# Latent scores in three products of high and low parts, and casts in slot order at two feed-forward fronts

## What is computed

```python
def _attend_blocks(q, k, v):            # q: 512 x 16 x 96, k: 768 x 16 x 96
    scale = QK_HEAD_DIM ** -0.5
    def one(qblk):                      # 128 queries
        s = jnp.einsum('bqhd,bkhd->bhqk', qblk, k, preferred_element_type=jnp.float32) * scale
        p = jax.nn.softmax(s, axis=-1).astype(v.dtype)
        return jnp.einsum('bhqk,bkhv->bqhv', p, v)
    ...
def _conv_ffn(h, w_up, conv_w, conv_b, w_down):
    gate, val = jnp.split(h @ w_up, 2, axis=-1)
    return (jax.nn.silu(_dwconv3(gate, conv_w, conv_b)) * val) @ w_down
```

## Time and profile before

| | |
|---|---|
| median of 3 runs | 3225.2 us (3224.78 to 3226.74) |
| the profiled execution | 3222.23 us |
| its span in the trace | 3220.4 us |
| PE busy | 3148.1 us, 98% |
| DVE, ACT, POOL busy | 62%, 46%, 43% |
| latent items | 997.6 to about 1230 us of the span |

### The profile page before, as it was taken

How to read it: one execution, slowest core, us unless ns; L and a number is a source line. 1 busy time by engine, 2 the same in 40 slices (tenths; PEclk the granted TensorE clock), 3 DMA queues, 4 the chain that set the end, 5 groups by cost and what they waited for, 6 DMA issues and landing times.

```text
span 3220.4 us, 45656 instructions
## 1 busy us (share of the span) xinstructions
PE 3148.1 (98%) x18262; PEld 2618.2 (81%) x18262; DVE 2003.2 (62%) x3212; ACT 1483.0 (46%) x2689; POOL 1382.0 (43%) x800
## 2 busy tenths in 40 slices
PE   7999999999999999999999999999999999989998
PEld 4876888888875557899986888899997788869997
DVE  5877366323337663877735685388873678368885
ACT  4323422222246774555544535455553544445554
POOL 2221423232254445355552234646555234435555
PEclk9999999999999999999999999999999999999999
DMA  7333334122132002223332120423333121213331
GB/s 272 109 97 120 126 101 151 56 63 69 50 118 103 14 14 88 90 92 105 112 122 75 47 67 34 129 79 100 104 118 107 44 71 45 63 57 105 100 99 68
DMA packets 89408, 288.53 MB, mean 90 GB/s; under 512 B 10187, under 2 KB 13835, under 8 KB 88428
## 3 DMA queue, kind: packets, MB, share of 16 engines
q1 hardware_dynamic: 89196, 285.60, 27.6%
HBM read 283.47 MB, written 2.10 MB: 89 GB/s over the span
## 4 chain that ended last, share of the span: by engine, by line
PE 82%; DVE 6%; issue 4%; POOL 4%; ACT 3%; DMA 1%; SPq 0%; POOLq 0%; DVEq 0%; ACTq 0%
PE ps L613 13%; PE ps L616 13%; PE ps L614 13%; PE ps L3432 6%; PE ps L3434 5%; PE ps L3433 5%; PE ps L672 2%; PE ps L674 2%; PE ps L673 2%; PE ps L2254 2%; POOL WL L561 1%; PE ps L3106 1%; DMA ring<-in_w_mod 1%; POOL T L904 1%; PE ps L2697 1%
## 5 line engine op out<-in xcount | busy, mean ns | idle before, releaser
L561 POOL TENSOR_TENSOR WL<-ring,WH 128x1024 fp32r<-128x1024 f32 (+4 forms) x477 | 975.2, 2050 | 1331.5 <-ACT WH L551 1331.5
L551 ACT CAST WH<-ring 128x1024 fp32r<-128x1024 f32 (+4 forms) x524 | 462.6, 884 | 442.1 <-PE ps L616 287.8
L613 PE MATMUL ps<-FR,WH 128*128 128x512 f32 x1120 | 419.5, 375 | 0.3
L614 PE MATMUL ps<-FR,WH 128*128 128x512 f32 x1120 | 410.2, 373 | 0.0
L616 PE MATMUL ps<-FR,WL 128*128 128x512 f32 x1120 | 389.2, 373 | 0.0
L613 PE MATMUL ps<-HX,WH 128*128 128x512 f32 x744 | 294.3, 396 | 0.0
L616 PE MATMUL ps<-HX,WL 128*128 128x512 f32 x744 | 292.7, 393 | 0.0
L614 PE MATMUL ps<-HX,WH 128*128 128x512 f32 x744 | 291.2, 391 | 0.0
L3432 PE MATMUL ps<-XH,WH 128*128 128x256 f32 x912 | 260.4, 285 | 10.5 <-ACT ps L3583 7.9
L3433 PE MATMUL ps<-XL,WH 128*128 128x256 f32 x912 | 258.7, 284 | 0.0
L3434 PE MATMUL ps<-XH,WL 128*128 128x256 f32 x912 | 258.6, 284 | 0.0
(11 more groups left out here) (465 smaller groups left out, 7480.4 us busy)
## 6 DMA issues: line engine op xcount, KB each, us to landing
ring<-in_ffn_w_up SPq DMA_DIRECT2D x88, 512.0 KB, 3.7
ring<-in_w_up SPq DMA_DIRECT2D x88, 512.0 KB, 3.7
ring<-in_w_mod SPq DMA_DIRECT2D x64, 512.0 KB, 4.4
ring<-in_w_in_tok SPq DMA_DIRECT2D x40, 512.0 KB, 3.7
ring<-in_w_mod_columns SPq DMA_DIRECT2D x32, 512.0 KB, 4.4
ring<-in_w_in_feat SPq DMA_DIRECT2D x32, 512.0 KB, 3.6
ring<-in_w_down SPq DMA_DIRECT2D x48, 320.0 KB, 4.0
ring<-in_ffn_w_down SPq DMA_DIRECT2D x40, 320.0 KB, 3.0
```

The source lines that it names most:

```text
L551: act.copy(WH[:, p % SPLITS, 0:n], src).then_inc(*split.a.up("high", p))
L561: pool.tensor_tensor(WL[:, p % SPLITS, 0:n], unit_source(p)[0], WH[:, p % SPLITS, 0:n], ALU.subtract).then_inc(*low_up(split.g, p))
L613: pe.matmul(o, high, xh, first, False)
L614: pe.matmul(o, high, xl, False, False)
```

## The change

Two changes that don't touch each other come together.

**Scores.** QT and KT become F32R, and hold the high parts. QL and KL, the low parts of the queries and keys of one batch, lie in the slots of WH and WL (all three of WL, two of WH). The one float32 product becomes three F32R products. ACT now casts queries and the first 512 keys of every head (`head_high`), DVE the last 256 keys, and DVE makes all three low parts (`head_low_v`), from PSUM and the high part. Since the slots are taken, `ring.upto` keeps the units of w_o from being asked for until step (11, 0), i = 51; three are cast by ACT at i = 64 and made low by POOL behind the last scaling, and PE's pieces of w_o move to (15, 0) and (15, 2), i = 67 and 69.

**Fronts.** In both early feed-forwards the unit of group 5 is made low by DVE instead of POOL (in `between(2)`), ACT's casts of units first + 6 to first + 8 move forward, and the rest and sums of (3) and (4) change places with the taps on DVE.

```diff
         in_vector |= {g_.last for t_ in (L_ffn1, *L_ffb) for g_ in (*t_.groups[3:5], *t_.groups[-8:])}
-        in_vector.add(L_ffb[1].groups[2].last)
+        in_vector |= {L_ffb[1].groups[2].last, L_ffb[1].groups[5].last, L_ffn1.groups[5].last}
...
-        QT = [buf(7360, 4, 512), buf(15680, 4, 512)]
-        KT = [buf(9408, 4, 768), buf(17728, 4, 768)]
+        QT = [nc.alloc_sbuf_tensor_at(f"QT{x}", [128, 4, 512], F32R, offset=base + 4 * o)
+              for x, o in enumerate((7360, 15680))]
+        KT = [nc.alloc_sbuf_tensor_at(f"KT{x}", [128, 4, 768], F32R, offset=base + 4 * o)
+              for x, o in enumerate((9408, 17728))]
+        QL = WH[:, :, :].rearrange("p a b -> p (a b)")[:, 0:2048].rearrange("p (a b) -> p a b", a=4)
+        KL = WL[:, :, :].rearrange("p a b -> p (a b)").rearrange("p (a b) -> p a b", a=4)
         VT = [buf(5824, 6, 256), CX[:, :, :].rearrange("p a b -> p (a b)")[:, 0:1536].rearrange("p (a b) -> p a b", a=6)]
         OT = buf(20800, 8, 512)
...
+            ring.upto = L_a.groups[-1].last + 1
...
-                cast_to(act, g.last + 2)
+                cast_to(act, min(g.last + 2, L_a.groups[-1].last))
...
-            cast_to(act, g.last + 3)
...
-            for g in L_a.groups:
-                rest_to(pool, g.last + 2)
-            rest_to(pool, g.last + 3)
+            rest_to(pool, L_a.groups[-1].last)
...
-        def heads_evict(eng, copy, W, n, h, odd):
-            for x, (src, ts, dst) in enumerate(turns(h)):
-                if (3 * h + x) % 2 == odd and (n or x):
-                    eng.wait_ge(*mla.pe.at("turn", n, h, x))
-                    copy(dst(n % 2), ps("turn", n, h, x)[0:96, 0:len(ts) * 128]).then_inc(
-                        *bank.emptied(("turn", n, h, x), W))
+        LAST_OF = (5, 7, 13, 15)
+
+        def head_high(eng, copy, W, n, h, x):
+            ts, dst = turns(h)[x][1:3]
+            eng.wait_ge(*mla.pe.at("turn", n, h, x))
+            copy(dst(n % 2), ps("turn", n, h, x)[0:96, 0:len(ts) * 128]).then_inc(*W.up("head high", n, h, x))
+
+        def head_low_v(dve, n, h, x):
+            ts, dst, lo = turns(h)[x][1:4]
+            if n:
+                dve.wait_ge(*att.pe.at("scores", 16 * n - 16 + LAST_OF[h], 1))
+            else:
+                dve.wait_ge(*split.pe.at("used", L_a.groups[-1].last))
+            dve.wait_ge(*(mla.a if x < 2 else mla.v).at("head high", n, h, x))
+            dve.tensor_tensor(lo, ps("turn", n, h, x)[0:96, 0:len(ts) * 128], dst(n % 2), ALU.subtract).then_inc(
+                *bank.emptied(("turn", n, h, x), mla.v))
 
...
             for h in range(4):
-                heads_evict(act, act.copy, mla.a, n, h, 1)
-                mla.a.mark("made", n, h)
+                for x in range(n == 0, 2):
+                    head_high(act, act.copy, mla.a, n, h, x)
...
+            if n == 0:
+                for h in range(4):
+                    head_low_v(dve, 0, h, 0)
             yield
             for h in range(4):
-                heads_evict(dve, dve.tensor_copy, mla.v, n, h, 0)
+                for x in range(n == 0, 2):
+                    head_low_v(dve, n, h, x)
+                head_high(dve, dve.tensor_copy, mla.v, n, h, 2)
+                head_low_v(dve, n, h, 2)
...
             c0, c1 = CUTS[j]
             pe.wait_ge(*mla.v.at("made", n, h))
-            pe.wait_ge(*mla.a.at("made", n, h))
             b = bank.take_in(f"scores{j}", "ls", i, j)
             pe.wait_ge(*bank.free("ls", i, j))
-            pe.matmul(PS[b][:, 0:c1 - c0], QT[n % 2][0:96, h, t * 128:t * 128 + 128], KT[n % 2][0:96, h, c0:c1], True,
-                      True).then_inc(*att.pe.up("scores", i, j))
+            o, rows_ = PS[b][:, 0:c1 - c0], slice(t * 128, t * 128 + 128)
+            pe.matmul(o, QT[n % 2][0:96, h, rows_], KT[n % 2][0:96, h, c0:c1], True, False)
+            pe.matmul(o, QT[n % 2][0:96, h, rows_], KL[0:96, h, c0:c1], False, False)
+            pe.matmul(o, QL[0:96, h, rows_], KT[n % 2][0:96, h, c0:c1], False, True).then_inc(*att.pe.up("scores", i, j))
 
...
                     bank.release("scores0")
                     bank.release("scores1")
-                if v >= 14 and part == 0:
+                if (v, part) == (11, 0):
+                    ring.upto = None
+                    ring.ask(ring.p + SPLITS)
+                if (v, part) in ((15, 0), (15, 2)):
                     next(out)
                     bank.kept.update(bank.place[L_o.name, g.key, 0] for g in L_o.groups[:2])
...
+                else:
+                    act.wait_ge(*att.pe.at("scores", 63, 1))
+                    cast_to(act, L_o.groups[2].last)
...
+                if i == 64:
+                    rest_to(pool, L_o.groups[2].last)
```

The fronts:

```diff
-            if not L.early:
+            if L.early:
+                between(2)
+            else:
                 between(0)
                 between(1)
             low(2)
...
                 center(0, 1)
+            if L.early:
+                cast_to(act, first + 6)
             gate_silu(0)
+            if L.early:
+                cast_to(act, first + 7)
             for n in range(1, FRONT):
                 if n >= 2:
                     high(n - 2)
                     if L.early:
-                        cast_to(act, first + 7)
+                        cast_to(act, first + 8)
                 center(n, 0)
                 gate_silu(n)
...
-            sums_1_2(FRONT + 1)
+            if not L.early:
+                sums_1_2(FRONT + 1)
             for n in range(FRONT):
                 for val in range(2):
                     key = (name, ("up", 2 * n + val), 0)
                     if not val or L.val_conv:
                         taps(n, val, ps(*key), key, T[:, 2 * val + n % 2, :])
-                    if n == (1 if L.early else FRONT - 1) and not val:
+                    if n == FRONT - 1 and not val and not L.early:
                         rest_v(dve, L.unit["1 2", FRONT])
                         sums_3_4(FRONT)
                 dve.wait_ge(*fw.v.now())
...
                         *bank.emptied(key, fw.v, "gated", name, n, 0))
+                if n == 0 and L.early:
+                    rest_v(dve, L.unit["1 2", FRONT])
+                    sums_3_4(FRONT)
                 if 1 <= n < FRONT - 1:
                     low(n - 1)
+                    if L.early:
+                        sums_1_2(FRONT + 1)
             for i in range(FRONT, FT + 1):
                 j = i - 1
                 if FRONT < i < FT:
```

More of the change, by code:

```diff
@@ L213, in start @@
     def start(self):
-        self.n, self.p, self.asked, self.cast, self.rest = 0, 0, 0, 0, 0
+        self.n, self.p, self.asked, self.cast, self.rest, self.upto = 0, 0, 0, 0, 0, None
     def raw(self, src, n, parts=128, kept=False):
@@ L234, in ask @@
     def ask(self, upto):
-        while self.asked < min(upto, len(self.splits)):
+        while self.asked < min(upto, len(self.splits) if self.upto is None else self.upto):
             src, n = self.splits[self.asked]
@@ L2035, in turns @@
         def turns(h):
-            return [(qtok, range(4), lambda g: QT[g][0:96, h, :]),
-                    (ktok, range(4), lambda g: KT[g][0:96, h, 0:512]),
-                    (ktok, range(4, 6), lambda g: KT[g][0:96, h, 512:768])]
+            return [(qtok, range(4), lambda g: QT[g][0:96, h, :], QL[0:96, h, :]),
+                    (ktok, range(4), lambda g: KT[g][0:96, h, 0:512], KL[0:96, h, 0:512]),
+                    (ktok, range(4, 6), lambda g: KT[g][0:96, h, 512:768], KL[0:96, h, 512:768])]
         def batch(x):
@@ L2092, in turned_heads_pe @@
         def turned_heads_pe(pe, n, h, x, what):
-            src, ts, dst = turns(h)[x]
+            src, ts = turns(h)[x][0:2]
             b = bank.take("turn", n, h, x)
@@ L2133, in heads_a @@
                 for h in range(4):
-                    act.wait_ge(*mla.pe.at("turn", 0, h, 0))
-                    act.copy(turns(h)[0][2](0), ps("turn", 0, h, 0)[0:96, :]).then_inc(
-                        *bank.emptied(("turn", 0, h, 0), mla.a))
+                    head_high(act, act.copy, mla.a, 0, h, 0)
             yield
             for h in range(4):
-                heads_evict(act, act.copy, mla.a, n, h, 1)
-                mla.a.mark("made", n, h)
+                for x in range(n == 0, 2):
+                    head_high(act, act.copy, mla.a, n, h, x)
                 yield
```

## The result

The changed kernel takes 3250.5 us (median of 4 runs, 3250.2 to 3254.1), the kernel before 3225.0 in the same comparison: ratio 1.0082, 95% interval 1.0070 to 1.0094. It is slower by 25.5 us, where the forecast was +19.6 and 3245.

A forecast was written before the change was run, and what follows sets the result against it. The latent stage was taken as bound by PE, busy 98% of the span. Terms -16.3 + 29.5 + 3.8 + 1.7 + 4.8 + 0.9 - 4.8 = +19.6 on 3225.2 gave 3245 us, range 3226 to 3262.

The forecast's parts named there:

- part 2: Items that make a head: DVE, ACT, DVE become a loop of 5.85 us an item; over three batches +29.5 us.
- sum pair: DVE's sum of the item before, queued behind the subtractions, counted as the last 0.25 us of the head items' loop.
- the hold: In the head items' loop, POOL's scaling delays DVE's combined maximum, which takes 0.59 us, 0.37 of it from contention.
- part 1: Latent score products: three F32R products replace the float32 pair, saving 0.255 us an item on PE, 64 times, -16.3 us.
- part 3: Start of the latent items: batch 0's casts and subtractions precede item 0, +3.8 us; half clock behind PE's idle, +1.7.
- part 4: End of the latent items: w_o waits for POOL's low parts and a moved piece comes later, +4.8 us; half clock, +0.9.
- part 5: Early fronts: the wait for POOL goes, the copy's wait grows; copies come 3.0 and 3.5 us earlier, -4.8 us altogether.
- The heads were not absorbed: Rival for the head items: PE has enough work ahead to hide the loop, part 2 is nil, 3215.5 us; chance 0.10.
- the F32R products of an item: Rival for the scores: three F32R products take as long as the float32 pair, part 1 is nil, 3261 us; chance 0.05.
- PE's clock did fall in the head items: Rival: half clock in the head items adds 2.4 to 13.2 us, middle 8, three times, giving 3269 us; chance 0.09.

## Why the prediction was right, point by point

**The loop** (part 2) was right as a mechanism and, to a few hundredths, in size: 5.85 us an item counted, 5.85 measured, and 5.85 + 6.00 + 6.33 + 5.85 = 24.03 from item 28 to 32 where 24.0 stood. What PE gets back behind it was put at 1.0 and is 1.3 (item 17 at 1.83 us instead of 3.16). The three head stages, items 12 to 17 of each batch, cost 8.5 us net in the trace; the sum had 9.8 less the saving of five items, 8.5. Taking the sum pair and the hold out of the loop shortened it by just what they last (0.26 and 0.38), and taking the exponentials out left an item at DVE's own work.

**The scores** (part 1) are the term that was mis-sized. Each item that PE sets saves 0.25, as counted (3.16 to 2.91). But it was multiplied by 64. The ledger gives -0.6 for items 2 to 12 of the first batch, -1.5 for the eleven items between the head stages, twice, and -2.4 for the last fourteen: -6.0, where these 46 items should give -11.7. The step that failed is "on PE and so on the path, 64 times", and it rests on reading 60.88 of 61.90 us as a stage that PE binds throughout. Of the 5.7 that are missing, 3.2 are missing in items 9 to 12 of the three batches that make heads: items 10 to 12 are DVE's, before and after, and PE's products could be shortened to a third there without moving them. The other 2.5 are spread: the second item behind a head stage saves nothing (5.74 to 5.79), and the last fourteen items save 2.4 where 3.6 were counted. What sets those no run isolates.

The ledger's parts, heads 25.5, scores -6.0, start 5.2, end 5.2 and fronts -2.9, add up to +27.0 where the sum had 19.6; the medians moved by 25.5. The scores are 5.7 of the difference and the fronts 1.9; 0.8 is the counted saving of the three items that these parts leave out, and the other parts missed by 0.5 or less each, the other way.

**The start** (part 3): first maximum 3.3 later was counted, and 3.2 is left of 7.6 once the 1.7 and 2.7 ahead of it are taken off. PE's idle time of 4.2 and the half clock behind it came as said; the third maximum is 2.0 later again. 5.2 against 5.5 of the sum. That moving the heads can't mend it was not foreseen: the expectation of that run was wrong.

**The end** (part 4): +5.2 in the ledger, 5.7 in the sum. The parts differ. A rest of POOL took 2.34 there, not 2.05, the wait for it was only 1.6, and 1.3 us came as a wait for DVE's low part of the output (L2367) that the moved piece had covered. The half clock did not come behind the wait for POOL, where PE was at 1.00, but ahead of it, from 1255.6 on, behind this wait of 1.3 and one of 0.7; 3.0 us at 0.50 cost some 1.5.

**The fronts** (part 5): that the removed waits would come back in the wait for the copy was right. Sizes: in the first front PE's first instruction behind the copy comes 2.0 earlier than in the trace of before (against item +34.4, +32.4), counted 3.0, and 2.0 are lost again to half clock, counted 1.7: 0 instead of -1.3. In the second front -2.9 instead of -3.5. Alone the fronts gave -2.5 with an interval from -6.8 to -0.6, which holds both figures. The forecast of 4 to 6 us for the one wait was right for the first front, 5.3, and wrong for the second, 8.2: the whole first wait, and the 1.4 us by which PE comes sooner at full clock, are added to the second.

**The rivals.** The heads were not absorbed, and the F32R products of an item stand with 1.06 us in the chain of waits (0.24 + 0.23 + 0.23 and 3 x 0.12), where 1.03 was counted. PE's clock did fall in the head items, which had a chance of 0.09, but it cost next to nothing. The argument against it, that rows 14 show half clock behind idle times of over 3 us only, misread them: the first of those stretches, with 0.51, stands behind an idle time of 2.8. By stretch, the third of these items in the first two stages (items 14 and 30):

```profile
1061.20:1067.53 6.33, 3.43 (x26) 2.29 (x24) 3.79 (x10) 3.71 (x9) 1.47 (x1) 1.00 0.00 0
```

```profile
1130.11:1136.44 6.33, 4.50 (x23) 3.42 (x23) 3.79 (x10) 3.71 (x9) 1.47 (x1) 0.77 0.00 0
```

With the clock at 1.00 and at 0.77 the item takes the same 6.33 us; only PE's share of it grows, 3.43 to 4.50, at the expense of its idle time. The loop of DVE and ACT hides it, as the low end of that rival had it. The rule named with it (the Trainium skill, TensorE: Matmul & The Clock Gate, A second HAM failure mode) is borne out in that the clock swings between its two levels when PE idles between groups; in the kernels with the casts first, where PE idles less, the same stage stays at 1.00. The loss of throughput that the page adds is not seen here.

## What to carry to other kernels

When an operation that waited for PE alone is made to wait for another engine, look at what stands ahead of it there, and what waits for it behind: here a 0.57 us cast behind exponentials that wait for the same DVE closed a loop of 5.85 us where 3.5 were needed, and one exchange on ACT gave 21 us back. A loop like this could be priced from durations before it existed, here to a few hundredths of a microsecond, by adding the rows around it once. Before a saving is multiplied by the number of its items, read the distance between items: those where another engine is the bound save nothing, and a busy share of 98% over the whole batch hides them.

## What the runs showed of the hardware

- POOL's tensor_tensor with two operands in SBUF holds a DVE instruction that has two of its own until it is done: 0.20 us became 1.47, 0.94 became 2.22, 0.22 became 0.59. The one that started first holds the other: where DVE's of 0.94 us had started 0.16 ahead, POOL's took 2.10 instead of 1.47. DVE's reductions from PSUM and its subtractions of an SBUF operand from PSUM (0.67 and 0.68 us) beside the same POOL instruction were not held.
- PE's clock fell to half behind single idle times of 4.2, 5.3 and 8.2 us, and behind 1.3 and 0.7 us close together at the end of the items. In the head items, with idle times of 1.5 to 2.4 us one after another, it fell in some items and not in others of the same make (1.00 in item 14, 0.77 in item 30). Before, it stayed at full level behind one of 2.9 us and fell behind another of 2.8. So the same idle time doesn't always end the same way, and half a stretch, some 2 us, should be kept in the range for each.
